# The end of a matrix memory's output moved into the features of the next mixer, with four key lines on GpSimd instead of ScalarE

## What is computed

```
# mLSTM, end: h = num / max(|den|, exp(-m)), both directions
h = h * rsqrt(mean(h * h, axis=-1) + eps) * mlstm_norm_g
y_b = sum(h, over the two directions)            # then gated, transposed to the grid

# RWKV-7 features, for the context and then for the latents
decay = exp(-exp(-softplus(-(w0 + tanh(wd) @ w_up)) - 0.5))
a     = sigmoid(a0 + ad @ a_up)
kk    = kk / max(norm(kk), 1e-12)
k_eff = k * (1 + (a - 1) * k_a)                  # the "key line"
# scan, per token: S = S * w - (S kk) (kk a)^T + v k^T
```

## Time and profile before

| | us |
|---|---|
| median of 3 runs | 2667.61 |
| lowest, highest | 2666.59, 2672.57 |
| the profiled execution | 2667.66 |
| its span in the profile | 2665.9 |
| TensorE busy | 2519.4 |
| VectorE busy | 1309.2 |
| ScalarE busy | 1020.5 |
| GpSimd busy | 850.1 |

### The profile page before, as it was taken

How to read it: one execution, slowest core, us unless ns; L and a number is a source line. 1 busy time by engine, 2 the same in 40 slices (tenths; PEclk the granted TensorE clock), 3 DMA queues, 4 the chain that set the end, 5 groups by cost and what they waited for, 6 DMA issues and landing times.

```text
span 2665.9 us, 53106 instructions
## 1 busy us (share of the span) xinstructions
PE 2519.4 (95%) x19732; PEld 2078.4 (78%) x19732; DVE 1309.2 (49%) x2662; ACT 1020.5 (38%) x1725; POOL 850.1 (32%) x689
## 2 busy tenths in 40 slices
PE   7999669699999989999999999989999999999997
PEld 3885469499967867887888888878888888888886
DVE  5765655656553327997444444400044444444443
ACT  4222453533352233223666666632322322232222
POOL 2420243444554445645555555524400000000001
PEclk8999889799999999999999999999999999999999
DMA  6541000000032324234355444464455555555551
GB/s 263 188 174 40 1 2 1 2 0 0 1 145 89 94 71 143 85 100 144 115 205 181 169 169 169 169 236 142 134 196 197 190 189 189 191 196 196 194 197 64
DMA packets 163913, 348.64 MB, mean 131 GB/s; under 512 B 13368, under 2 KB 79416, under 8 KB 161664
## 3 DMA queue, kind: packets, MB, share of 16 engines
q1 hardware_dynamic: 163840, 347.65, 37.7%
HBM read 276.30 MB, written 71.30 MB: 130 GB/s over the span
## 4 chain that ended last, share of the span: by engine, by line
PE 53%; DVE 5%; issue 1%; DMA 1%; POOL 1%; ACT 1%; SPq 0%; DVEq 0%; ACTq 0%; POOLq 0%
PE ps_a L85 9%; PE ps_a L86 9%; PE ps_a L87 9%; PE ps_y L85 7%; PE ps_y L86 7%; PE ps_y L87 7%; PE ps_w L2535 4%; DVE cand L2328 0%; DVE top_ix L2311 0%; DMA w_scratch<-w_block 0%; DVE top_ix L2324 0%; DVE scores_left L2314 0%; DVE picked L2385 0%; DVE pick L2369 0%; DVE pick L2152 0%
## 5 line engine op out<-in xcount | busy, mean ns | idle before, releaser
L2711 DVE TENSOR_TENSOR v_lo<-v_raw,v_hi 128x1024 fp32r<-128x1024 f32 x128 | 158.3, 1237 | 542.2 <-ACT v_hi L2663 542.2
L85 PE MATMUL ps_a<-h_hi,u_hi 128*128 128x512 f32 x1024 | 412.0, 402 | 8.2 <-ACT act L2056 7.7
L86 PE MATMUL ps_a<-h_hi,u_lo 128*128 128x512 f32 x1024 | 405.7, 396 | 0.0
L87 PE MATMUL ps_a<-h_lo,u_hi 128*128 128x512 f32 x1024 | 405.7, 396 | 0.0
L2663 ACT ACTIVATE v_hi<-v_raw 128x1024 fp32r<-128x1024 f32 x128 | 135.8, 1061 | 478.4 <-PE ps_a L87 470.0
L85 PE MATMUL ps_y<-gated_hi,v_hi 128*128 128x512 f32 x768 | 299.5, 390 | 3.1 <-DVE gated_lo L2713 3.1
L87 PE MATMUL ps_y<-gated_lo,v_hi 128*128 128x512 f32 x768 | 299.3, 390 | 0.0
L86 PE MATMUL ps_y<-gated_hi,v_lo 128*128 128x512 f32 x768 | 299.2, 390 | 0.0
L2056 ACT ACTIVATE act<-ps_a 128x512 f32<-128x512 f32 x128 | 76.5, 597 | 414.0 <-PE ps_a L87 397.4
L85 PEld LDWEIGHTS ps_a<-h_hi,u_hi 128*128 128x128 f32 x1024 | 194.0, 189 | 52.4 <-issue 8.5
L2699 POOL TENSOR_TENSOR v_raw<-v_raw 128x512 f32<-128x512 f32 x6 | 7.7, 1288 | 711.7 <-ACT v_raw L2683 711.7
(11 more groups left out here) (524 smaller groups left out, 5417.4 us busy)
## 6 DMA issues: line engine op xcount, KB each, us to landing
u_raw<-in_uT SPq DMA_DIRECT2D x128, 512.0 KB, 3.6
v_raw<-in_v SPq DMA_DIRECT2D x128, 512.0 KB, 4.8
a_scratch<-act SPq DMA_DIRECT2D x128, 256.0 KB, 2.1
w_scratch<-w_block SPq DMA_DIRECT2D x8, 4096.0 KB, 12.2
w_ring<-w_scratch SPq DMA_DIRECT2D x64, 512.0 KB, 4.4
gated<-a_scratch SPq DMA_DIRECT2D x128, 256.0 KB, 4.8
mg_raw<-in_w_merge SPq DMA_DIRECT2D x36, 512.0 KB, 3.6
vM<-in_ada_rows SPq DMA_DIRECT2D x32, 512.0 KB, 4.9
```

What stands on the lines that cost most here:

```text
L85: pe.matmul(out, wh, xh, start=first, stop=False)
L86: pe.matmul(out, wl, xh, start=False, stop=False)
L87: return pe.matmul(out, wh, xl, start=False, stop=last)
L2711: v.tensor_tensor(vl[:, q], v_raw[:, q], vh[:, q], ALU.subtract).then_inc(v_lo, 1)
```

## The change

- The division, squares and sums of the last chunk of each direction, and all of the memory's end behind them, leave `phase_mlstm` and are woven into the context's features. Direction 0 is scaled by sixteen ScalarE copies instead of four VectorE instructions. `ssq`, `dn` and the gain get a home that outlives the memory (`MemoryEnd`).
- Features and scan share one block, for the context and for the latents; the meeting of all engines between them is gone, and waits on semaphores stand in its place (`ScanEntry`).
- The key lines of z = 1 are on GpSimd, behind those of z = 0.
- `w65` is one buffer for each direction; the clearing in between is gone.
- The first inverses are made in the features, tile by tile, as eight instructions of 128x64 in place of two of 128x256.
- TensorE waits for the step q ahead of a q product and for the step k ahead of a k product.

```diff
@@ phase_rwkv_features, ScalarE
+            if end is not None:
+                for z in range(2):
+                    act.wait_ge(end.divided, z + 1)
+                    act.activation(square[:, z], outer(z), ACT.Square).then_inc(end.squared, 1)
...
-                if z == 1:
-
-                    act.wait_ge(slot_done, 2)
...
-                if z == 1:
-                    act.wait_ge(a_done, n + 1)
-                    act.activation(b.ke[:, z, c, 0:T], b.qa[:, z, c, 0:T], ACT.Identity, bias=ka[:, 1, c:c + 1],
-                                   scale=ka[:, 0, c:c + 1]).then_inc(line_act, 1)
...
+                        for i in range(n_x):
+                            for h in range(MH):
+                                m = act.activation(y[:, 0, i, h * DV:(h + 1) * DV], hc[:, 0, i, h, 0:DV], ACT.Copy,
+                                                   scale=end.ssq[:, 0, i, h:h + 1])
+                            m.then_inc(end.scaled0, 1)
+                if n == PAIRS and end is not None:
+                    act.wait_ge(end.turned, 1)
@@ TensorE
+                if n == PAIRS and end is not None:
+                    pe.wait_ge(norm_max, 1)
+                    for i in range(n_x):
+                        pe.wait_ge(end.summed, i + 1)
+                        for h in range(MH):
+                            mm = pe.transpose(ps_n[h][:, i * MC:(i + 1) * MC], y[:, 0, i, h * DV:(h + 1) * DV], b.ident[:])
+                    mm.then_inc(end.turned, 1)
                 project(n)
@@ GpSimd
+            for c in range(PAIRS):
+                g.wait_ge(a_done, PAIRS + c + 1)
+                g.tensor_scalar(b.ke[:, 1, c, 0:T], b.qa[:, 1, c, 0:T], ka[:, 0, c:c + 1], ka[:, 1, c:c + 1], ALU.mult,
+                                ALU.add).then_inc(line_act, 1)
@@ VectorE
-            v.wait_ge(scanned, PAIRS)
-            v.memset(w65[:, :, :, C:C + 1], 0.0).then_inc(slot_done, 1)
-            v.wait_ge(slot_done, 2)
...
             for n in range(PAIRS, 2 * PAIRS):
                 decay(n)
+                m = inverse(0, n - PAIRS)
...
                 rates(n)
...
+                m = inverse(1, n - PAIRS)
@@ phase_rwkv_scan, GpSimd, first chunk
+                if first:
+                    g_.wait_ge(entry.scanned, (g + 1) * PAIRS)
+                    g_.wait_ge(entry.normed, (g + 1) * PAIRS)
+                    g_.wait_ge(entry.line_act if g else entry.line_pool, PAIRS)
@@ phase_rwkv_scan, TensorE
+                        prep_s[g].wait(pe, i, "k" if k else "q")
                         if k == 0:
-                            prep_s[g].wait(pe, i, prep_names[-1])
```

More of the change, by code:

```diff
@@ L530, in rwkv_masks, with __init__, sem, phase_rwkv_features @@
     return np.concatenate([out, out], 0)
-def phase_rwkv_features(nc, a, b, f, T, tag):
+class ScanEntry:
+    def __init__(self, nc, b, tag, ginv):
+        def sem(name):
+            return b.semaphore(nc, name + tag)
+        self.ginv = ginv
+        self.gi_s = [Steps(sem(f"rws_gi{g}"), ["gi"]) for g in range(2)]
+        self.scanned, self.normed = sem("rwf_scanned"), sem("rwf_normed")
+        self.line_pool, self.line_act = sem("rwf_line_pool"), sem("rwf_line_act")
+def phase_rwkv_features(nc, a, b, f, T, tag, block, entry, end=None):
     nch = T // C
@@ L544, in phase_rwkv_features @@
         ka = sb("rw_ka" + tag, [P, 2, PAIRS])
-        w65 = sb("w65" + tag, [P, PAIRS, nch, C + 1])
+        w65 = [sb(f"w65_{z}" + tag, [P, PAIRS, nch, C + 1]) for z in range(2)]
         first = sb("w65_first" + tag, [P, nch, C + 1])
@@ L611, in _ @@
         def _(g):
+            if end is not None:
+                for z in range(2):
+                    g.tensor_tensor(outer(z), outer(z), end.dn[:, z, chunk(z)].unsqueeze(2).to_broadcast([P, MH, DV]),
+                                    ALU.mult).then_inc(end.divided, 1)
             g.wait_ge(half_done, 1)
@@ L650, in rates @@
                                        op1=ALU.mult).then_inc(normed, 1)
+            if end is not None:
+                for z in range(2):
+                    v.wait_ge(end.squared, z + 1)
+                    v.tensor_reduce(end.ssq[:, z, chunk(z)], square[:, z], AX.X, ALU.add).then_inc(end.reduced, 1)
             for c in range(PAIRS):
@@ L721, in phase_rwkv_scan @@
         level_s = [Steps(sem(f"rws_level{g}"), [f"m{s}" for s in LEVELS]) for g in range(2)]
-        gi_s = [Steps(sem(f"rws_gi{g}"), ["gi"]) for g in range(2)]
+        gi_s = entry.gi_s
         copy_s = [Steps(sem(f"rws_copy{g}"), copy_names) for g in range(2)]
@@ L991, in inverse @@
                 gi_s[g].mark(v.reciprocal(ginv[g][:], b.G[:, g, :, bass.ds(start_of(n, g, C + 1, 1 - g), C)]))
-            for g in range(2):
-                gi_s[g].start(v)
-                inverse(0, g)
             def body(i, more):
@@ L1487, in _ @@
             g.tensor_copy(neg_r[32:LOW], blank).then_inc(gaps, 1)
-            for n in range(2 * n_x):
+            for n in range(2 * n_x - 2):
                 i, z = n // 2, n % 2
@@ L1601, in _ @@
                 unit(n)
-            for n in range(n_x):
-                pe.wait_ge(summed, n + 1)
-                for h in range(MH):
-                    out = (ps_s + ps_e)[h]
-                    mm = pe.transpose(out[:, n * MC:(n + 1) * MC], y[:, 0, n, h * DV:(h + 1) * DV], b.ident[:])
-            mm.then_inc(turned, 1)
         @block.scalar
@@ L2818, in build_program @@
                     b.m_mask = later("m_mask", [P, 2, MC])
-                    b.mlstm_g = later("mlstm_g", [P, MH])
                     b.win_v = later("win_v", [P, KT, MH * DV])
```

151 lines of the change are left out of this document (94 added, 57 removed).

## The result

The changed kernel took 2727.56 us (median of 4), before 2670.09 on the same chip: a ratio of 1.0214 with an interval of 1.0194 to 1.0235. Forecast were 2661.8 and a range from 2656.3 to 2667.3. The profiled execution took 2727.62 us, its span is 2725.8.

What follows compares the result with a forecast made beforehand. The prediction took the VectorE and ScalarE chain before each scan's second first-product, with TensorE waiting, as the bound; 2667.66 less 4.5 (context) and 1.3 (latents) gave 2661.9, stated as 2661.8 us, range 2656.3 to 2667.3.

Steps and rivals of the forecast that it cites:

- rival D: Scan loops on TensorE: passes lose their smooth run, about 2 us each over eight passes, 2678 us; chance 0.06.
- From that point on the scan's own chain is unchanged: Each scan, from TensorE's second first-product (direction 1, chunk 0) on: nothing changes.
- The sum: Whole kernel: 2667.66 less 4.5 us for the context and 1.3 for the latents, 2661.9, stated as 2661.8.
- 501.3: Latents' features: time in us at which the last scan and inverse end, before GpSimd's steps to the second product.
- the context's roots: Context features: both roots, after one shared pair of table loads, stand 11.35 us behind the features' start.
- A: Whole kernel: GpSimd instructions each hold VectorE up 0.25 us in the latents; 2661.8 us, 2659.8 to 2663.8; chance 0.42.
- B's price: Second direction: GpSimd's steps slip in without holding VectorE; 3.0 us less in latents, 1.5 in context, 2657.3; chance 0.28.
- C: Second direction: GpSimd instructions cost VectorE their whole length, 2666.8 us; signs: lines 1.5 us and more, rates over 1; chance 0.24.
- The moved wait: TensorE's queue in the scan: q products wait for q instead of k; weighed at nothing.
- The lines: Second direction's key lines, taken off ScalarE onto GpSimd: worth nothing by themselves, since VectorE is late next.
- The memory's end: Ahead of the context features: moving it takes 17.7 us off, of which 13.2 are given back by the second product.
- the block's start: Latents: gone between features and scan, along with a joint inverse of 1.75 us and direction 1's wait behind GpSimd.

Runs made afterwards that it cites:

- the runs with 72 signals: Changed kernel with 72 idle semaphore signals on TensorE behind the last projection of the latents' features, ahead of the latents' loop: 2686.48 us.
- with 4 behind the loop: Changed kernel with 4 idle semaphore signals on TensorE behind the latents' loop, at the end of its last, straight pass: 2729.69 us.
- the runs with 72, 96 and 128 signals: Changed kernel with that many idle semaphore signals on TensorE ahead of the latents' loop: 2686.48, 2681.30 and 2688.70 us.

## Why the prediction was wrong

- **The step that failed** is rival D's dismissal: "the loop grows by two waits only, and nothing in it is moved". With it fails "From that point on the scan's own chain is unchanged". The latents' loop doesn't change by one instruction (1729 in both traces, and the context's grows by one); it is moved as a whole, by four places, and its place counts. D had named the mechanism (the loop passes lose their smooth run because TensorE's code shifts) with a chance of 0.06 and a price of 2 us a pass. Measured: 11.5 us a pass (68.7 over six), in the latents alone. The price came from the last pass in straight code, where the code of the next piece comes while the current one runs. At the jump back nothing covered the fetch: TensorE stood for 3.5 to 6.8 us.
- **The sum was right for what it counted.** With the loop at its old place the kernel took 0.9968 of before, 8.5 us less, with 5.8 forecast, just inside the interval of 5.6 to 11.7. By trace: context 5.2 (forecast 4.5), latents 1.7 (1.3), together 6.9. The good figure for the latents is luck in part: the profiled execution lost 1.15 us there to TensorE's clock and before's didn't. At the clock that before had, the latents gain 2.9 (40.0 less the 37.1 of the runs with 72 signals and with 4 behind the loop), over twice the forecast, and both together 8.1. The sum has small slips too: 501.3 and its steps behind it give 507.6, not 507.4, so 1.1 for the latents; and the context's roots add up to 11.41, not 11.35.
- *Context.* The features' start came 1.30 us behind the last factor, as forecast (317.48 less 316.18). Behind the start: roots at 11.65 (11.35), ScalarE's copies 4.78 us (4.3), GpSimd's scalings done at 17.05 (17.2), last transpose at 24.6 (24.3), direction 0's last inverse 35.5 (36.55), second product 40.6 (41.25).
- *An inverse of 128x64* takes 0.52 us and 0.45 to the next start; estimated were 0.55 and 0.49.
- *Latents.* Direction 0's last inverse ended 32.05 behind the features' start (32.6), the second product came at 38.3 (38.7), although TensorE's clock cost this execution 1.15 us ahead of it; where it stayed up, 30.9 and 37.1. So GpSimd's steps held VectorE up less than A had it: from scan to scan a unit takes 2.65 to 2.85 us there, not 3.35. B's price (2.85) fits this stretch. Behind the inverse it is the other way: 6.27 us to the second product, where A's steps give 6.28 and B had taken 1.05 off. C is out, but one of its signs came: the four lines on GpSimd took 1.2 to 2.2 us (median 1.93), well over the 1.5 named, beside rates of 0.67 to 0.75 and only one over 1 (1.09). It was mostly GpSimd that was held up there, and VectorE little.
- *The moved wait* was "weighed at nothing", and as the cause of the loss it is nothing. But it brings 0.9 us at the start of each scan, 1.8 in all. The sum had this in it without saying so: it counts GpSimd's steps up to q, where the product before waited for k as well.
- *The lines* were weighed at nothing too, and nearly rightly: GpSimd's cost 0.8 us in the latents that ScalarE's don't.
- *The memory's end* was thought the main thing; it brings 2.4 by the traces. The shared block brings 6.5, which the prediction had as a remark ("the block's start").

## What to carry to other kernels

Ahead of any other forecast of a change on an engine with a long loop, count the loop's machine instructions and their place in the code: an edit outside it can move it across a boundary, and the price is then paid in pass after pass. The page shows it in one line, the packets of the instruction queue; here 48 against 102. A loop that fits only at some places should be shortened or placed on purpose: the changed kernel with four idle signals is faster than both kernels.

## What the runs showed of the hardware that was not expected

- 1729 instructions of TensorE loop freely where they end within seven pieces of 16 KB; from 5 to 32 instructions into the eighth, every other pass takes 36 to 38 us in place of 29.2, at 61 to 64 four of six passes 34 to 37, and from 65 on every pass 35 and more. In the runs with 72, 96 and 128 signals a fetched pass was followed by a free one where its last packet ended up to 1.9 us ahead of the jump back, and by a fetched one from 1.95 us on.
- A fetched pass brings nine pieces and costs 4 to 12 us. A piece takes 0.9 us and more as a packet, but TensorE stands 3.5 to 6.8 us at the jump.
- 128 idle semaphore signals in TensorE's queue delayed the changed kernel's second product in the latents by 5.2 us and 192 by 15, four and 32 by nothing, since TensorE waits there anyway.
- The mean granted clock of the 5.5 us behind the latents' features' start was 0.69 or 1.00 for the same instructions in different executions, and the kk multiplication and the scan came 1.15 us later where it was 0.69.
